# The merge gates' projection as three products of rounded operands, and the first token half running ahead from the out-projection into the feed-forward layer

## The reference

```
h   = rms_norm(x) * (1 + scale) + shift            # same for ctx
p   = h @ w_in                                     # RWKV part | GLA part | 2 x 2048 merge gates
y_r = rwkv7(p[:RWKV]);  y_g = gla(p[GLA])          # two token mixers on the same h
m   = sigmoid(p[gate_r]) * y_r + sigmoid(p[gate_g]) * y_g
x   = x + gate1 * rms_norm(m @ w_out)
h2  = modulate(rms_norm(x))
x   = x + gate2 * rms_norm((silu(h2 @ w_gate) * (h2 @ w_up)) @ w_down)
```

## Time and profile before

| | |
|---|---|
| median of 3 runs | 2163.39 us (2159.5 to 2163.41) |
| profiled execution | 2161.05 us |
| its span | 2159.3 us |
| mean granted clock of PE | 0.978 |
| busy: PE, DVE, ACT, POOL | 94%, 58%, 37%, 12% |
| gate matmuls of `phase_gla` that the page groups | 512 instructions, 113.4 us, 379 ns each |
| `phase_gla` | 579.7 to 769.7 us |
| `phase_rwkv_pre` | 773.2 to 924.2 us |
| out-projection ends, n = 4 of the feed-forward layer begins | 1400.0 us, 1442.1 us |

### The profile page before, as it was taken

How to read it: one execution, slowest core, us unless ns; L and a number is a source line. 1 busy time by engine, 2 the same in 40 slices (tenths; PEclk the granted TensorE clock), 3 DMA queues, 4 the chain that set the end, 5 groups by cost and what they waited for, 6 DMA issues and landing times. The chain is left out here.

```text
span 2159.3 us, 35926 instructions
## 1 busy us (share of the span) xinstructions
PE 2020.6 (94%) x15475; PEld 1651.2 (76%) x15475; DVE 1245.3 (58%) x1150; ACT 808.1 (37%) x895; POOL 249.9 (12%) x125
## 2 busy tenths in 40 slices
PE   5899999999999989967889899999999999999998
PEld 3367888888788866656788688778888888888886
DVE  3355666665556347768888486554445455444445
ACT  2232111212263235445554465443334333433333
POOL 0023121312304034301000020000000000000000
PEclk9899999999999999989999999999999999999999
DMA  8988889887554389967442678536555555555553
GB/s 305 382 284 313 315 316 322 290 318 270 153 143 124 88 233 312 297 151 195 93 92 57 113 228 323 178 98 192 184 187 194 186 185 192 194 202 192 193 195 115
DMA packets 355505, 453.62 MB, mean 210 GB/s; under 512 B 106062, under 2 KB 261054, under 8 KB 338094
## 3 DMA queue, kind: packets, MB, share of 16 engines
q1 hardware_dynamic: 347760, 440.59, 64.4%
q10 hardware_dynamic: 7614, 11.10, 1.4%
HBM read 413.43 MB, written 38.22 MB: 209 GB/s over the span
## 5 line engine op out<-in xcount | busy, mean ns | idle before, releaser
L220 DVE TENSOR_TENSOR f_w_lo<-t_w_raw,f_w_hi 128x2048 fp32r<-128x2048 f32 x132 | 302.4, 2292 | 361.5 <-ACT f_w_hi L214 361.5
L214 ACT ACTIVATE f_w_hi<-t_w_raw 128x2048 fp32r<-128x2048 f32 x132 | 252.9, 1916 | 436.0 <-PE pf L2926 288.0
L2924 PE MATMUL pf<-f_w_hi,h 128*128 128x512 f32 x704 | 276.3, 392 | 1.5 <-DVE h L2745 1.5
L2925 PE MATMUL pf<-f_w_lo,h 128*128 128x512 f32 x704 | 274.8, 390 | 0.0
L2926 PE MATMUL pf<-f_w_hi,h 128*128 128x512 f32 x704 | 274.7, 390 | 0.0
L214 ACT ACTIVATE p_w_hi<-h_w_raw 128x2048 fp32r<-128x2048 f32 x48 | 89.3, 1910 | 333.2 <-DVE stage L761 252.1
L906 DVE SCALAR_TENSOR_TENSOR late_acc<-h_of_x,siluc,late_acc 128x2048 f32<-128x2048 f32 x60 | 160.6, 2677 | 46.9 <-DMA h_of_x<-in_ada_w 45.2
L2975 PE MATMUL d_out<-f_w_hi,hid 128*128 128x512 f32 x704 | 176.3, 390 | 0.3 <-DVE f_w_lo L220 0.3
L264 PE MATMUL p_in<-h,p_w_hi 128*128 128x512 f32 x448 | 174.3, 389 | 0.0
L266 PE MATMUL p_in<-h,p_w_lo 128*128 128x512 f32 x448 | 174.3, 389 | 0.0
L265 PE MATMUL p_in<-h,p_w_hi 128*128 128x512 f32 x448 | 174.3, 389 | 0.0
(11 more groups left out here) (419 smaller groups left out, 3404.9 us busy)
## 6 DMA issues: line engine op xcount, KB each, us to landing
h_of_x<-in_ada_w SPq DMA_DIRECT2D x64, 1024.0 KB, 5.6
h_w_raw<-in_w_in SPq DMA_DIRECT2D x48, 1024.0 KB, 7.6
t_w_raw<-in_ffn_w_gate SPq DMA_DIRECT2D x44, 1024.0 KB, 5.2
t_w_raw<-in_ffn_w_up SPq DMA_DIRECT2D x44, 1024.0 KB, 5.2
t_w_raw<-in_ffn_w_down SPq DMA_DIRECT2D x44, 1024.0 KB, 4.9
h_w_raw<-in_ada_w SPq DMA_DIRECT2D x32, 1024.0 KB, 10.5
gate_w<-in_w_in SPq DMA_DIRECT2D x30, 1024.0 KB, 6.0
t_w_raw<-in_w_out SPq DMA_DIRECT2D x16, 1024.0 KB, 6.0
```

The costliest lines, as they stand in the source:

```text
L214: act.activation(self.hi[:, m % self.S, 0:w], self.raw[:, s, 0:w], ACT.Copy)\
L220: eng.tensor_tensor(self.lo[:, m % self.S, 0:w], self.raw[:, s, 0:w], b32(self.hi[:, m % self.S, 0:w]), ALU.subtract)\
L2924: pe.matmul(o, h2[:, 0, k, rows], fring.hi[:, s, at], start=k == 0, stop=False)
L2925: pe.matmul(o, h2[:, 0, k, rows], fring.lo[:, s, at], start=False, stop=False)
```

## The change

The token input `h` stays resident as hi and lo, context and latent apart (`[P, 2, 2, KT, SEQ]`), and `h_of_x`, its sum, is not made any more (one addition on POOL, one on DVE). The products of `phase_w_in` thereby read their 512 tokens as two runs of 256. Gates are made from 64 parts of 128x1024 (two output tiles wide, four blocks deep), five raw buffers, three for hi. Each part is split: hi on ACT (60) or DVE (4), lo on POOL (50) or DVE (14), lo in the place of the raw part. Each block is three fp32r matmuls of 256 columns. `phase_gla` makes parts 0 to 35, 96 blocks of them ahead of level 0 (before: 112), 16 per level, 64 after; `phase_rwkv_pre` parts 36 to 61, 48 blocks ahead, 16 per pair, 32 after; the scan parts 62 and 63. A hi waits until the part three before it is used up. Outputs and norm of `phase_gla` run head by head.

In `phase_mix` half 0 is normalised, turned and split during the out-projection of half 1, turned ahead of its last group; the feed-forward layer starts with half 0 on tiles 0 to 3, with tiles 2 and 3 split to buffers apart, and POOL copies half 0 to its final place.

```diff
 class Gates:
...
+    STAGES, RAW, SPLIT = 4, 5, 3
+    AHEAD = KT * P // (GATE_W // 2)
+    HI_VECTOR = [4, 5, 6, 7]
+    LO_VECTOR = [0] + list(range(13, 28, 2)) + [37, 39, 41, 61, 63]
...
+        if n >= self.SPLIT:
+            eng.wait_ge(self.used, n - self.SPLIT + 1)
+
+    def hi(self, act, n):
+        assert n not in self.HI_VECTOR
+        self.wait_raw(act, n)
+        act.activation(self.high[:, n % self.SPLIT], self.place(n), ACT.Copy).then_inc(self.hi_scalar, 1)
...
+    def lo(self, eng, n):
+
+        eng.wait_ge(*self.hi_done(n))
+        eng.tensor_tensor(self.low_place(n), self.place(n), b32(self.high[:, n % self.SPLIT]), ALU.subtract)\
+           .then_inc(self.lo_done(n)[0], 1)
...
-            mm = pe.matmul(self.banks[t % nb][:, 0:SEQ], tiles[:, slot, k * P:(k + 1) * P], self.hx[:, k, :],
-                           start=k == 0, stop=k == KT - 1)
...
+            last = self.mm3(pe, self.banks[(f - self.first) % nb][:, 0:SEQ], self.high[:, n % self.SPLIT, cols],
+                            self.low_place(n)[:, cols], self.h[:, 0, k, :], self.h[:, 1, k, :], k == 0,
+                            k == KT - 1)
...
                 for j in range(PAIRS):
                     b = j % 2
+                    gates.lo(pool, 44 + 2 * j)
...
+                    gates.lo(pool, 45 + 2 * j)
                     if j + 2 < PAIRS:
                         neighbours(j + 2)
...
                     act.activation(nrm[:, b, :], nrm[:, b, :], ACT.Sqrt).then_inc(s_nrm, 1)
-                    for t in finished(j):
-                        gates.copy(act, t)
+                    gates.hi(act, 45 + 2 * j)
                     if j + 2 < PAIRS:
                         middle(j + 2)
+                    if j % 2 == 0:
+                        gates.copy(act, 20 + j)
+                        gates.copy(act, 21 + j)
+                    gates.hi(act, 46 + 2 * j)
...
-                gates.multiply(pe, KT * inner, KT * (gates.tiles - inner))
+                gates.multiply(pe, 8 * PRE_PARTS + 48 + 16 * PAIRS, 32)
...
                 for n in range(LEVELS):
+                    gates.lo(pool, 12 + 2 * n)
                     pool.wait_ge(s_e, 2 * n + 1)
                     pool.tensor_tensor(E[:, n % 2, 0], k[:], E[:, n % 2, 0], ALU.mult).then_inc(s_K, 1)
...
-                gates.multiply(pe, 96, 16)
...
-                    gates.multiply(pe, 112 + 14 * n, 14)
+                    gates.multiply(pe, 96 + 16 * n, 16)
...
+                pe.wait_ge(s_og, 5)
+                for n in range(4):
+                    if n == 3:
+                        turn(1)
+                    fring.wait_split(pe, n, n)
+                    pe.wait_ge(s_hlo0, n + 1)
+                    for k in range(KQ * n, KQ * n + KQ):
+                        last = ffn(n, 0, k, True)
+                last.then_inc(s_fg, 1)
+                for n in range(4):
+                    pe.wait_ge(s_hlo1, n + 1)
+                    for k in range(KQ * n, KQ * n + KQ):
+                        last = ffn(n, 1, k, True)
+                    last.then_inc(fring.used, 1)
+                pe.wait_ge(s_h0, 1)
```

More of the change, by code:

```diff
@@ new lines, in __init__, with begin @@
+        self.hi_scalar, self.hi_vector = new(name="gate_w_hi_by_scalar"), new(name="gate_w_hi_by_vector")
+        self.lo_gpsimd, self.lo_vector = new(name="gate_w_lo_by_gpsimd"), new(name="gate_w_lo_by_vector")
+        self.used, self.made = new(name="gate_w_used"), new(name="gate_first_of_two_made")
+        self.copied = new(name="gate_copied")
+        self.stored = [new(name=f"gate_stored{n}") for n in range(self.STAGES)]
+    def begin(self, first, banks):
+        self.first, self.banks = first, banks
@@ new lines, in copy @@
+    def copy(self, act, f):
+        if f % 2 == 0 and f < 2 * KT - 2:
+            act.wait_ge(self.made, f // 2 + 1)
+        else:
+            act.wait_ge(self.used, 1 + max(n for n, part in enumerate(GATE_PARTS) if part[0] <= f))
+        if f >= self.STAGES:
+            act.wait_ge(self.stored[f % self.STAGES], 16 * (f // self.STAGES))
+        act.activation(self.stage[:, f % self.STAGES], self.banks[(f - self.first) % len(self.banks)][:, 0:SEQ], ACT.Copy)\
+           .then_inc(self.copied, 1)
@@ L1101, in _ @@
                 load(1)
[L1102 to L1104 removed]
+                for n in range(41, 47):
+                    gates.load(sp, n)
+                gates.store(sp, 18)
+                gates.store(sp, 19)
                 for j in range(PAIRS):
@@ L2760, in _ @@
-                h_lo(KT // 2 - 1)
+                for g in range(4):
+                    h_of(1, g)
+                    if g:
+                        h_lo(g - 1)
+                h_lo(3)
                 def silu(n, b):
@@ L2900, in _, with turn @@
                         three(k, 0, c)
+                def turn(b):
+                    pe.wait_ge(s_diag, b + 1)
+                    if b:
+                        pe.wait_ge(s_hb, KT)
+                    for k in range(KT):
+                        last = pe.matmul(pT[k // 4][:, k % 4 * P:(k % 4 + 1) * P], x[:, b, k * P:(k + 1) * P], diag[:, b, :],
+                                         start=True, stop=True)
+                        if k % 4 == 3:
+                            last.then_inc(s_T, 1)
                 for b in range(2):
                     for c in range(4):
+                        if (b, c) == (1, 3):
+                            turn(0)
                         for k in range(KT - 2 if b == 0 else KT - RAW, KT):
```

725 lines of the change are left out of this document (442 added, 283 removed).

## The result

The changed kernel takes 2220.61 us (median of 4 runs, 2218.79 to 2222.39), the kernel before 2163.26 (4 runs, 2159.5 to 2163.41): ratio 1.0266, 95% interval 1.0246 to 1.0285. The direction was forecast, but not the size: +57 us and not +17, outside the range. The profiled execution took 2220.62 us.

A forecast was written before the change was run, and what follows sets the result against it. PE was taken to bound GLA's levels and tail, the other engines' chain the pairs; afterwards DVE and POOL queue as one. Terms -2 + 12 - 6 + 24 + 0 - 11 = +17 on 2161.05 gave 2178 us, range 2140 to 2199.

The forecast's parts named there:

- The price of a block: Gates on PE: three products of 256 columns take 0.355 us a block instead of 0.431.
- the tail: GLA after the levels: 64 cheaper blocks and outputs made head by head give -6 us (-3 to -6.5).
- w_in: Products of phase_w_in reading two runs of 256: same time, 0 us, up to +7 possible.
- The levels: GLA's eight levels: the queue of DVE and POOL sets 9.3 us a level instead of 7.83, +12 us.
- the first rival: Whole kernel: the shared queue of DVE and POOL doesn't bind, -18 us, 2143; chance 0.27.
- Head ... I take -2: GLA before level 0: 16 blocks leave, others get cheaper, decays stand bare behind one POOL lo; -2 us (-4 to +2).
- Head of `phase_rwkv_pre`: Before pz of pair 0: a hi, a lo and 8 blocks after the last lora_x, +6 us (0 to +8).
- The pairs: phase_rwkv_pre: POOL's lo ahead of ks delays DVE's chain by 2.3 us a pair, +16 us for 7 periods.
- the second lo ... I take 0: Pairs of phase_rwkv_pre: it may meet sh and the last dr, 0 to 1.3 us; taken as 0.
- No gate matmul is a link of that chain: Pairs of phase_rwkv_pre: the post-to-post chain of 14.38 us holds no gate product, so PE's saving gives nothing back.
- The end of the phase: phase_rwkv_pre after the last pair: 32 blocks instead of 16, partly beside the last stores, +2 us (0 to +4).
- Out-projection: Out-projection to feed-forward layer: half 0 running ahead fills PE's waits, -11 us (-8 to -15).

The follow-up runs named there:

- run 5: Changed kernel with the lo of parts 12, 14 to 26 in GLA's levels on DVE instead of POOL: 2217.47 us.
- run 1: Changed kernel with POOL's two lo per pair of phase_rwkv_pre held back, one until DVE's last ks, one until the previous pair's last dr: 2202.93 us.
- run 9: Changed kernel with POOL's lo of tile 3 and its copy of half 0 held until DVE's additions for half 1 are done: 2210.12 us.
- run 4: Changed kernel with the eight gate blocks between turning and states in GLA's head put ahead of the turning, in both directions: ratio 1.0271 to the kernel before.
- run 2: Changed kernel with DVE's four hi of parts 4 to 7 in GLA's head moved behind the four foldings: 2218.83 us.
- run 6: Changed kernel with the load of part 37 issued ahead of SP's wait for GLA's result: 2215.85 us.
- runs 7, 8: Changed kernel, phase_rwkv_pre's head: parts 39 to 41 ahead of LoRA inputs, 2214.03 us; also copies of tiles 18 and 19 ahead of hi 41, 2221.15 us.

## Why the prediction was right in direction and wrong in size

- **The price of a block** (0.355 us taken, 0.359 measured), **the tail** (-6; -6.2) and **w_in** (0; 0) held.
- **The levels** (+12; +11.2): the one queue of DVE and POOL was reckoned at 9.3 us a level; four of the eight lie 9.1 to 9.6 apart, and run 5 shows the mechanism. That the sum fits is in part luck: the first two are longer (10.2 and 11.4), the last two shorter (7.6 and 7.5).
- **The Trainium skill** was cited for this lock, page "SBUF — State Buffer", section "Who interferes with whom"; the first rival was that it would not bind in single pairs. The trace agrees with the rule: `ks` at 2.46 us beside the lo and 0.42 without (run 1). The same section counts `tensor_scalar` among the operations that can take the shared ports, and that agrees too: `o_diag`, of that kind, took 2.40 us beside POOL's lo (run 9) and 0.29 without.
- **"Head ... I take -2"** failed: +11.1 in these two executions. I looked at what left the head and took for its price one POOL lo. What the runs show in its place: the first lo ahead of the first gate (2.4), eight blocks inside the chain between turning and states, in each direction (turning to states 5.36 and 6.25 us for 1.83, run 4), and DVE's wait of 6.52 us for a part in the middle of the foldings (run 2). The order in which the blocks stand on PE was to be read from the changed code, and I did not. How the rest of the 11.1 divides stays open: the head scatters by 6 us with the granted clock.
- **The hand-over** (+8.2) was missing from the sum. "The loads get longer runs, which helps the queues; no wait for them is on the chain" was the step: SP's load of part 37 stands behind its wait for GLA's result (2.9 of the 8.2, run 6), and the `vp` products take 10.4 us for 4.27 beside three lo. The prediction applied the lock to the levels and the pairs, and not to this stretch.
- **Head of `phase_rwkv_pre`** (+6; +13): a hi, a lo and 8 blocks from the last `lora_x` was too simple; parts, bank copies and mixing on three in-order engines were each in the way of the next (runs 7, 8). Which of the remaining us belongs to which is not settled.
- **The pairs** (+16; +23.6): the lo ahead of `ks` was right (14.7; run 1 wins 15 by moving both lo). The term set to zero, "the second lo ... I take 0", was mis-sized: 4.3. "No gate matmul is a link of that chain" failed too: in the changed kernel `pss` comes late behind gate products, and DVE's last `dr` with it (4.9). And `nb` beside `ks` (1.3) was not in the sum. The end of the phase (+2; +3.6) lay in its range.
- **Out-projection** (-11; -3.8, and -1.3 ahead of it): "One lo's 4.6 us is what I let through" failed. The lo and the copy stand one behind the other under the four additions, 10.86 us instead of 2.74. Run 9 wins 6.8 of it back. "32 turning ones at 0.11" was misread: the trace of before has 64 PE instructions there, two for each product, and the turning of one half takes 3.84 us (x32 in run 9), not 1.8.
- **PE's granted clock** (0.77 and 0.78 in head and pairs; 0.92 and 1.00 before) was named only as an addition to a rival. In the pairs it rose to 0.87 in run 1, where the waits fell; that it follows from the waits is not shown. In the head the same code came out 6 us apart at 0.77 and 0.86. Why one execution has the longer spell at the lower of the two levels (1.2 and 2.4 GHz) stays open, as does why the scan's length scatters by some 12 us.

## What to carry to other kernels

Before counting what a cheaper product saves, find in each stage the chain that ends last; of the 39 us reckoned as saved on PE by the gates, at most the 6.2 of the tail arrived. DVE and POOL don't meet only through semaphores: `ks` took 2.46 us for 0.42 with no semaphore between it and the lo. So count their operations on SBUF as one queue wherever both work, and put POOL's under a reciprocal. And for each instruction that gets a new wait, list what stands behind it on its engine: here a load on SP, a bank copy on ACT and a folding on DVE.

## What the hardware showed that I had not expected

- POOL is held up as well, in work on one tensor: `u` took 1.31 us instead of 0.77 while DVE's `dr` of two operands ran.
- DVE's operations on one tensor are not safe either: `o_diag` took 2.40 us for 0.29 beside POOL's lo.
- The reciprocal was safe cover here: POOL's lo takes 2.36 us under its 3.35, and neither is longer (run 1).
